# Two transformer blocks on one core: the gate steps spread over four chunks, the second output projection in alternating PSUM pairs, casts first in the inverse's chunks

## The reference

```
proj = rmsnorm(h) @ w_in_2            # q, f, i, g of HGRN2; q, k, v, z, b, a of gated delta
o_a  = hgrn2(a_q, a_f, a_i, lb)       # f = lb + (1 - lb) sigmoid(z), cumulated log f inside chunks
qkv  = silu(causal_conv(b_q, b_k, b_v)); q, k = l2norm(q), l2norm(k)
beta = sigmoid(b_b); g = -exp(A_log) * softplus(b_a + dt_bias)
o_b  = gated_delta(q, k, v, beta, g)  # needs the inverse of a unit triangular matrix per head and chunk
mix  = [rmsnorm(o_a) * silu(a_g), rmsnorm(o_b) * silu(b_z)]
h    = h + mix @ w_out_2
h    = h + peer(rmsnorm(h))           # query, top 16 of product keys, 16384 experts, computed densely
```

## Time and profile before

| | |
|---|---|
| median of 3 runs | 3259.11 us (3258.15 to 3260.24) |
| the profiled execution | 3259.25 us, of which the span is 3257.5 us |
| mean granted clock of PE | 0.994 |
| PE busy | 3207.8 us, 98% of the span |
| PEld busy | 2862.8 us, 88% |
| DVE busy | 2030.7 us, 62% |
| ACT busy | 1470.3 us, 45% |
| POOL busy | 501.8 us, 15% |
| block 2 in the trace | about 1135 to 1719 us |

### The profile page before, as it was taken

One profiled execution on the slowest core, in us unless ns is written; L12 is line 12 of the kernel. 1 busy time (PEld: TensorE's weight loads), 2 busy tenths in 40 slices (PEclk: granted clock), 3 DMA queues, 4 the chain that ended last, 5 costly groups with the idle time before them and its releaser, 6 DMA issues.

```text
span 3257.5 us, 48209 instructions
## 1 busy us (share of the span) xinstructions
PE 3207.8 (98%) x19974; PEld 2862.8 (88%) x19974; DVE 2030.7 (62%) x1833; ACT 1470.3 (45%) x1289; POOL 501.8 (15%) x418
## 2 busy tenths in 40 slices
PE   8999999999999999999999999999999999999998
PEld 7788899999999878878879999999999888888886
DVE  5455665565555656766356888999974555555554
ACT  6564453344444363464435444555544433333333
POOL 0000000000000002226300000989940000000000
PEclk9999999999999999999999999999999999999999
DMA  7444465555555443343245566676776666556663
GB/s 272 155 155 159 164 225 192 193 193 193 193 192 191 146 168 124 122 156 116 91 155 214 200 214 220 225 250 235 249 259 248 238 244 252 227 230 258 234 243 116
DMA packets 132117, 644.18 MB, mean 198 GB/s; under 512 B 14720, under 2 KB 47872, under 8 KB 62848
## 3 DMA queue, kind: packets, MB, share of 16 engines
q1 hardware_dynamic: 96592, 624.08, 53.0%
q10 hardware_dynamic: 35376, 17.94, 1.9%
HBM read 606.31 MB, written 35.66 MB: 197 GB/s over the span
## 4 chain that ended last, share of the span: by engine, by line
PE 94%; DVE 3%; ACT 2%; issue 1%; DMA 1%; SPq 0%; DVEq 0%; ACTq 0%
PE pj L293 12%; PE pj L292 12%; PE pj L294 12%; PE pj L280 7%; PE pj L279 7%; PE pj L278 7%; PE pj L1743 3%; PE pj L1745 3%; PE pj L1744 3%; PE pj L877 3%; PE pj L879 3%; PE pj L878 3%; PE pt L280 2%; PE pm L280 2%; PE pm L279 2%; PE pt L279 2%
## 5 line engine op out<-in xcount | busy, mean ns | idle before, releaser
L260 ACT ACTIVATE hi<-raw 128x2048 fp32r<-128x2048 f32 x534 | 1023.4, 1917 | 1367.2 <-PE pj L294 640.7
L267 DVE TENSOR_TENSOR lo<-raw,hi 128x2048 fp32r<-128x2048 f32 x400 | 918.4, 2296 | 678.9 <-ACT hi L260 678.1
L292 PE MATMUL pj<-xh,hi 128*128 128x256 f32 x3328 | 919.9, 276 | 0.0
L293 PE MATMUL pj<-xl,hi 128*128 128x256 f32 x3328 | 918.8, 276 | 0.0
L294 PE MATMUL pj<-xh,lo 128*128 128x256 f32 x3328 | 918.8, 276 | 0.0
L293 PEld LDWEIGHTS pj<-xl,hi 128*128 128x128 f32 x3328 | 624.9, 188 | 0.6
L292 PEld LDWEIGHTS pj<-xh,hi 128*128 128x128 f32 x3328 | 624.7, 188 | 0.6
L294 PEld LDWEIGHTS pj<-xh,lo 128*128 128x128 f32 x3328 | 624.7, 188 | 0.0
L267 DVE TENSOR_TENSOR lo_in<-raw,hi 128x2048 fp32r<-128x2048 f32 x134 | 309.3, 2310 | 266.0 <-ACT hi L260 265.3
L2431 POOL TENSOR_SCALAR hotA<-cst,slotT 128x128 fp32r<-128x128 f32 x256 | 338.2, 1337 | 473.6 <-ACT slotT L2274 437.3
L1743 PE MATMUL pj<-hi,xh 128*128 128x512 f32 x576 | 236.5, 411 | 13.4 <-ACT proj L1812 7.3
(11 more groups left out here) (397 smaller groups left out, 4267.3 us busy)
## 6 DMA issues: line engine op xcount, KB each, us to landing
raw<-w_peer SPq DMA_DIRECT2D x256, 1024.0 KB, 6.3
raw<-w_mlp SPq DMA_DIRECT2D x128, 1024.0 KB, 4.8
raw<-w_in SPq DMA_DIRECT2D x102, 1024.0 KB, 4.8
raw<-w_out SPq DMA_DIRECT2D x32, 1024.0 KB, 4.8
raw<-w_q SPq DMA_DIRECT2D x16, 1024.0 KB, 4.9
act_scratch<-hidU SPq DMA_DIRECT2D x32, 512.0 KB, 2.9
gates_scratch<-stage ACTq DMA_DIRECT2D x8, 2048.0 KB, 17.0
hidV<-act_scratch SPq DMA_DIRECT2D x32, 512.0 KB, 3.7
```

The source lines that it names most:

```text
L260: nc.scalar.activation(hi[:, j, :], raw[:, j, :], ACT.Copy).then_inc(hi_ready, 1)
L267: nc.vector.tensor_tensor(low(q)[:, j, :], raw[:, j, :], hi[:, j, :].bitcast(F32), ALU.subtract).then_inc(lo_ready, 1)
L292: nc.tensor.matmul(o, hi[:, j, cols], xh[:, k0 + k, :], start=clears, stop=False, skip_group_check=True)
L293: nc.tensor.matmul(o, hi[:, j, cols], xl[:, k0 + k, :], start=False, stop=False, skip_group_check=True)
```

## The change

It moves steps between chunks, changes the order of steps inside chunks, and gives the second output projection a second PSUM pair.

- Gates: DVE's first gate step no longer waits for ACT's sigmoid but goes first. ACT loads one table set that holds Exp and Ln (`preload_act_table_set`) behind the sigmoid in k = 10 and does gate part 1 and the first logarithm there; masks and the second logarithm move to k = 12. DVE does gate part 1 and the first split at the top of k = 11, the second split at k = 13. PE waits for the last gate step (`g_step` 6) at the fourth HGRN step and not at the first.
- `K_TILE_FIRST` (k = 11 and 39): ACT evacuates tile 0 before it casts.
- L2 norms: all of them in k = 39, the sum before DVE's lo.
- Inverse (k = 49 to 56): ACT's cast and DVE's lo come first in the iteration; the evacuation of tile 0 comes behind the first copy of a level.
- Output projection 2: groups 3, 5 and 7 use `pj[0]`; from group 3 on PE waits for the sums of one group earlier. Part 2 of the lift comes at o = 6 and part 3 at o = 7 (PE), o = 7 and 8 (ACT, DVE); part 3 is turned in `pm`. `mix_dve` part 1 comes before DVE's lo of k = 61.
- The stages after it name the two pairs the other way round.

```diff
@@
-                return (pm, pm, pt, pj[0])[b]
+                return (pm, pm, pt, pm)[b]
@@ hgrn_pe, part 0 and 1
-                    pe.wait_ge(g_step, 6)
                 hg_step(i, ((2, products), (0, transposes), (0, decay_sums)))
             else:
+                if i == 3:
+                    pe.wait_ge(g_step, 6)
                 hg_step(i, ((3, sum_v),))
@@ gates
             if part == 0:
                 act.wait_ge(wt_out, 2)
+                act.wait_ge(g_step, 1)
...
                 dve.wait_ge(wt_out, 2)
-                dve.wait_ge(g_step, 1)
@@ block2_pe
+        def block2_pair(k):
+
+            return pj[0] if k < 4 or (k - K_IN2) // 2 in (3, 5, 7) else pj[1]
...
-                    ready = ((out2_first, o // 2), (out2_second, o // 2))
+                    before = o // 2 if o < 6 else o // 2 - 1
+                    ready = ((out2_first, before), (out2_second, before))
+                if o == 6:
+                    ready = ((f_dve, 3), (f_dve, 4))
...
-                if o == 7:
-                    pe.wait_ge(mg_step, 4)
-                    lift_pe(pe, 4, 2, proj2)
-                    lift_pe(pe, 4, 3, proj2)
+                if o in (6, 7):
+                    if o == 6:
+                        pe.wait_ge(mg_step, 4)
+                    lift_pe(pe, 4, o - 4, proj2)
@@ block2_act
                 if k == K_GATE + 1:
                     gates_act(act, n, 0)
-                if k == K_GATE + 2:
+                    nc.scalar.preload_act_table_set(LOG_EXP)
+                    gates_act(act, n, 1)
                     log_forget_act(act, n, 0)
+                if k == K_GATE + 3:
+                    masks_act(act)
                     log_forget_act(act, n, 1)
-                    masks_act(act)
-                    gates_act(act, n, 1)
...
-                if k == K_L2 + 1:
+                if k == K_L2:
                     l2_act(act, n)
...
+                    if i == 3 * (k - K_LEVEL) + 1 and k > K_LEVEL and k % 4 == 3 and k < K_IN2:
+                        evacuate(k // 4, 0)
...
+                inverse = K_LEVEL < k <= K_IN2
+                if inverse:
+                    c = Q_IN2 * SLOTS + k + 2
+                    make_hi(act, c // SLOTS, c % SLOTS)
                 if k % 4 == 0 and 8 <= k <= K_IN2:
                     evacuate(k // 4 - 1, 1)
...
-                if o in (8, 9):
-                    lift_act(act, 4, o - 6, head_gain, Q_OUT2 * SLOTS)
+                if o in (7, 8):
+                    lift_act(act, 4, o - 5, head_gain, Q_OUT2 * SLOTS)
...
+                if k in K_TILE_FIRST:
+                    evacuate(k // 4, 0)
@@ block2_dve
+                    gates_dve(dve, n, 0)
+                if k == K_GATE + 2:
+                    gates_dve(dve, n, 1)
+                    split_dve(dve, 0)
+                if k == K_L2:
+                    l2_dve(dve, n, 0)
...
-                if k == K_GATE + 1:
-                    gates_dve(dve, n, 0)
-                if k == K_GATE + 3:
-                    split_dve(dve, 0)
+                if k == K_GATE + 4:
                     split_dve(dve, 1)
-                    gates_dve(dve, n, 1)
...
-                if k in (K_L2, K_L2 + 1):
-                    l2_dve(dve, n, k - K_L2)
+                if k == K_L2:
+                    l2_dve(dve, n, 1)
...
+                if k == K_STATE + 3:
+                    mix_dve(dve, n, 1)
+                inverse = K_LEVEL < k <= K_IN2
+                if inverse:
+                    c = Q_IN2 * SLOTS + k + 2
+                    make_lo(dve, c // SLOTS, c % SLOTS)
                 if o in (-2, -1):
                     lift_dve(dve, 4, o + 2, head_gain)
...
-                if o in (8, 9):
-                    lift_dve(dve, 4, o - 6, head_gain)
+                if o in (7, 8):
+                    lift_dve(dve, 4, o - 5, head_gain)
@@ later stages
-        v_pair = [pt, pm, pj[0], pj[1]]
+        pq_ = [pj[1], pj[0]]
+        v_pair = [pt, pm, pq_[0], pq_[1]]
```

More of the change, by code:

```diff
@@ L43 @@
 NEG = -30000.0
+LOG_EXP = "natural_log_exp_and_others"
 W1 = 6 * H * HD
@@ L72 @@
 K_GATE, K_HGRN, K_CONV, K_L2, K_OPS, K_LEVEL, K_STATE = 9, 13, (33, 34, 35, 36, 37, 38, 40, 41, 42), 39, 43, 48, 58
+K_TILE_FIRST = (K_GATE + 2, K_L2)
 Q_END = Q_V + PEER_SB
@@ L1733, in dense @@
                 q, j, k0, first, last = block2_chunk(k)
-                pair = pj[0] if k < 4 else pj[1]
+                pair = block2_pair(k)
                 pe.wait_ge(lo_ready, q * SLOTS + j + 1)
@@ L1879, in block2_act @@
                     lift_act(act, 4, o + 2, head_gain, (Q_OUT2 - 1) * SLOTS + o + 3)
-                if o in (8, 9):
-                    lift_act(act, 4, o - 6, head_gain, Q_OUT2 * SLOTS)
+                if o in (7, 8):
+                    lift_act(act, 4, o - 5, head_gain, Q_OUT2 * SLOTS)
                 if o in (14, 15):
                     lift_act(act, 5, o - 14, column(S_GFFN), (Q_OUT2 + 1) * SLOTS + 3 + o - 14)
-                if k >= 1:
+                if k in K_TILE_FIRST:
+                    evacuate(k // 4, 0)
+                if k >= 1 and not inverse:
                     c = Q_IN2 * SLOTS + k + 2
                     make_hi(act, c // SLOTS, c % SLOTS)
-                if k % 4 == 3 and 4 <= k < K_IN2:
+                if k % 4 == 3 and 4 <= k < K_IN2 and not inverse and k not in K_TILE_FIRST:
                     evacuate(k // 4, 0)
@@ L1947, in beside @@
                     state_squares_dve(dve, n, 0)
-                if k in (K_STATE + 2, K_STATE + 3):
-                    mix_dve(dve, n, k - K_STATE - 2)
+                if k == K_STATE + 2:
+                    mix_dve(dve, n, 0)
             def add(o, t):
@@ L1957, in add @@
                 part = resid[:, t, g * NB:(g + 1) * NB]
-                nc.vector.tensor_tensor(part, part, pj[1][:, t, :], ALU.add).then_inc((out2_first, out2_second)[t], 1)
+                nc.vector.tensor_tensor(part, part, block2_pair(K_IN2 + o)[:, t, :], ALU.add).then_inc((out2_first, out2_second)[t], 1)
             for k in range(K_ALL):
@@ L2059, in query_pe @@
                         pe.wait_ge(tp_l, 4 * n + j + 1)
-                    multiply_up(pe, Q_WQ + g, j, pj[g % 2], 4 * j, j == 0, j == SLOTS - 1)
+                    multiply_up(pe, Q_WQ + g, j, pq_[g % 2], 4 * j, j == 0, j == SLOTS - 1)
                     if g == 0 and j == 0:
@@ L2075, in router_act @@
                     act.wait_ge(r_S, b - 1)
-                nc.scalar.activation(qT[b % 2][:, :, :], up_view(pj[b % 2]), ACT.Copy).then_inc(wq_evac, 1)
+                nc.scalar.activation(qT[b % 2][:, :, :], up_view(pq_[b % 2]), ACT.Copy).then_inc(wq_evac, 1)
             if j == 2:
@@ L2244, in up_block @@
                 for j in range(SLOTS):
-                    multiply_up(pe, s + Q_PEER, j, pj[par], 4 * j, j == 0, j == SLOTS - 1)
+                    multiply_up(pe, s + Q_PEER, j, pq_[par], 4 * j, j == 0, j == SLOTS - 1)
                     if is_block(s, 0) and j == 1:
@@ L2364, in scale_up @@
                     dve.wait_ge(u_out[par], (s - (2 + par)) * 8 + 16 if not isinstance(s, int) else 16 * (s // 2))
-                nc.vector.tensor_tensor(hidU[par][:, :, :], up_view(pj[par]), rs_rowU[:, :].unsqueeze(1).broadcast_to([P, 4, TT * P]),
+                nc.vector.tensor_tensor(hidU[par][:, :, :], up_view(pq_[par]), rs_rowU[:, :].unsqueeze(1).broadcast_to([P, 4, TT * P]),
                                         ALU.mult).then_inc(u_left, 1)
```

## The result

The changed kernel takes 3229.91 us (median of 5 runs, 3228.7 to 3230.61), the kernel before 3259.02 beside it (5 runs, 3258.15 to 3260.24): a ratio of 0.9909, 95% interval 0.9899 to 0.992. 3231 was forecast, with 3226 to 3239 as the range. The profiled execution has a span of 3228.1 us, against 3257.5.

The account below looks back on a forecast made before the run. PE, busy 98% of the span, was taken to bound the kernel, so only its stops cost time. Gates 12.7, L2 norms 2.7, inverse 3.0 and projection 10.0 sum to 28.4: 3259.1 - 28.4 = 3230.7, forecast 3231 us, range 3226 to 3239.

Parts of the forecast that it names:

- Gates, 12.7: Gate stretch, k = 12 to 13: all 12.7 us that PE loses there is gained, nothing is late next.
- the loads: Gates on ACT: four table loads become one; without the preload ACT is 2.6 us later, costing 0.5 us at most.
- L2 norms, 2.7: Around k = 40 to 42: 0.7 + 4.2 us lost turn into 2.2, gain 2.7, bounds 0 and 4.9.
- two new waits for cy: Transposes after the L2 norms: PE waits 1.1 us twice, in place of one wait of 2.3; clock stays up.
- Port contention: L2 stretch: DVE casts beside POOL lose 0.15 us in each of four steps, 0.6 us, inside the bounds.
- Inverse, 3.0 out of 3.4: k = 49 to 56: casts first bring copy and update earlier; gain 3.0 of 3.4 us lost, bounds 0 and 3.4.
- Output projection 2, 10.0: Second output projection: waits for adds and xl go, all 10.0 us gained, bounds 6 and 10.0.
- the spare times: Output projection 2: lo(63) is ready 2.4 us before PE wants it, mg_step 3.8 us before.
- New waits in the middle: L2 norms and inverse give nothing, or one lift still waits and lowers the clock: 3236 to 3240, chance 0.17.
- the gates kept their gain: Against the rival that the gate stretch only moves: half of 12.7 stays, 3237 us, chance 0.05.
- the third rival: Output projection 2: alternating pairs make PE pause and the clock fall from k = 62, up to 3286 us, chance 0.03.
- DMA was no limit: Against the rival that raw chunks become the limit once PE no longer pauses: within 0.2% of before, chance 0.04.

Follow-up runs that it names:

- before_again: The kernel before, unchanged, profiled a second time: 3255.0 us (one run).
- gates_only: The kernel before with the gate steps' part of the change alone: 3245.39 us, ratio 0.9962 to the kernel before.
- no_l2: The changed kernel with the L2 norms placed as in the kernel before: 3230.86 us, ratio 0.9919 to the kernel before.
- no_inverse: The changed kernel with the inverse's chunks in the old order, casts behind the level's work: 3232.44 us, ratio 0.9925 to the kernel before.
- late_mix: The changed kernel with `mix_dve` part 1 behind lo again in iteration k = 61: 3228.58 us, ratio 0.9909 to the kernel before.
- no_pairs: The changed kernel with one PSUM pair in output projection 2 and the old waits: 3236.04 us, ratio 0.9936 to the kernel before.

## Why the prediction was right, step by step

The time was right within 1.1 us. The sum of four terms, 28.4, came out as 30.45 in the traces, less the 1.0 by which `tail` happened to start later; the medians differ by 29.1. So part of the closeness is luck: all the three terms other than the gates were too small, by 2.1 us together, and the start of `tail`, which the change does not touch, took half of that back.

Two numbers of the working don't add up, and nothing hangs on them: the waits of the earlier trace rows give 20.7 us and not 20.5, and the forecast's own range, worked out from the stated bounds (22.7 to 31.0 us gained), is 3228 to 3236 and not 3227 to 3235.

**Gates, 12.7: measured 12.69**, in the full change and alone. The mechanism held: in the changed kernel ACT's rows stand where it put them, all about 1 us later as the trace is there:

```profile
1199.76 1.28 ACT L1850 ACT_TABLE_LOAD   x1
...
1202.85 1.06 ACT L1187 ACTIVATE split<-proj 128x1024 fp32r<-128x1024 f32 x1
1204.79 0.69 ACT L1822 ACTIVATE proj<-pj,stat 128x512 f32<-128x512 f32 x1 [0.87 <-PE pj L1752]
1205.37 1.90 ACT L262 ACTIVATE hi<-raw 128x2048 fp32r<-128x2048 f32 x1
1207.53 0.69 ACT L1822 ACTIVATE proj<-pj,stat 128x512 f32<-128x512 f32 x1 [0.26 <-PE pj L1752]
```

Both evacuations wait for PE, not PE for them. What each of the gate steps' moves is worth by itself was not run, but for the preload. What the prediction said of the loads was off: with the preload dropped ACT makes one more load in chunk 10, not two, and the cost is 0, where up to 0.5 was allowed for.

**L2 norms, 2.7: measured 3.0**, but made otherwise. The two new waits for cy were forecast and came, smaller: by starts 0.76 and 0.82 us and not 1.1 each (the list has 0.6 each). DVE's rows run in the order that the prediction followed, sum, lo, scalings, lo, taps:

```profile
1419.05 2.29 DVE L1403 TENSOR_REDUCE dn<-dsq 128x16 f32<-128x2048 f32 x1
...
1421.93 2.29 DVE L269 TENSOR_TENSOR lo_in<-raw,hi 128x2048 fp32r<-128x2048 f32 x1 [0.39 <-ACT hi L262]
...
1424.63 2.37 DVE L1411 TENSOR_TENSOR proj<-proj,dn 128x1024 f32<-128x1024 f32 x2
1426.91 2.29 DVE L269 TENSOR_TENSOR lo_in<-raw,hi 128x2048 fp32r<-128x2048 f32 x1
1429.11 2.43 DVE L1359 SCALAR_TENSOR_TENSOR cy<-pj,small,cy 128x255 f32<-128x255 f32 x6
```

The shorter wait at k = 40, for tile 0, is gone as forecast; a stop of 0.3 us stands in its place at the transposes of that chunk, which begin 0.51 behind the matmul before them where 0.23 is usual. The term counted the fall of the clock, 1.6 of the 3.0 us, as the L2 part's own, and that is not shown. The fall behind the 2.3 us wait stood in both traces with the gates' long stop (before, before_again) and in neither without it (gates_only, no_l2). Beside the gate steps' change the L2 part is worth 1.4. Two against two does not show that the long stop 230 us earlier is the cause, and by which mechanism it could be stays open.

**Port contention**, counted at up to 0.6 inside the bounds, went mostly the other way. One of DVE's casts, and POOL's steps beside it:

```profile
1433.83 2.40 DVE L269 TENSOR_TENSOR lo_in<-raw,hi 128x2048 fp32r<-128x2048 f32 x1 [2.29 <-ACT hi L262]
```

```profile
1433.72 0.60 POOL L1428 TENSOR_SCALAR dgS<-cst,gt 128x128 f32<-128x128 f32 x1
1434.30 2.40 POOL L1429 TENSOR_SCALAR dkb<-proj,gt 128x128 f32<-128x128 f32 x1
1436.68 0.60 POOL L1428 TENSOR_SCALAR dgS<-cst,gt 128x128 f32<-128x128 f32 x1
```

The cast took 2.40 instead of 2.29 and lost 0.11; POOL's step that began during it took 2.40 instead of 0.60 and lost 1.8. By the Trainium skill's rule of the shared port pair (SBUF — State Buffer, SBUF: two separate sides) the one that begins second stands until the other is done. POOL's step agrees with it. The cast does not: it began 0.11 behind a POOL step that had 0.49 to go, and lost only 0.11. No wait of PE for POOL is in the list.

**Inverse, 3.0 out of 3.4: measured 4.1 and 3.9** (against before, and by no_inverse). The mechanism was right and the size too small: the measured gain is over the upper bound of 3.4. The step that was off is "of 102.0 us PE is busy 98.6, so 3.4 lost": busy time runs to the modelled end of the last matmul and so covers part of each stop. Read by starts, the four stops add up to about 3.9, and all of them went.

**Output projection 2, 10.0: measured 10.67** against the first trace of before. The mechanism was right: no wait is left, and the spare times came out as worked out. The normalisation ended 4.0 us before PE wanted it (3.8 forecast) and lo(63) 2.5 us before (2.4 forecast). late_mix shows what the new place of `mix_dve` is worth, 0.79. Two parts of the 10.67 are not due to the change, or not always. About 0.6 is the 5.60 us pace of six chunks. About 3.2 of the other 10 is clock behind the two stops, which three of four traces with these stops have and one has not (81.95 less 78.77). Against before_again the same edit brings 6.9. Of the whole, the alternating pairs carry 6.4 (no_pairs, with 1.9 of clock and what follows in it). The lift in two parts was not taken back by itself, so what it is worth is not shown.

**The rivals.** New waits in the middle came, at 0.8 us each, and did not decide; the gates kept their gain; the clock stayed at 1.00 with the pairs alternating from group 3 on, so the third rival did not come true. The Trainium skill (TensorE: Matmul & The Clock Gate, A second HAM failure mode: psum-queue depth-cycling) tells of a kernel whose clock oscillated because PE idled shortly between groups of matmuls as it cycled PSUM banks; here PE had no idle time in the projection, and alternating the pairs alone did not bring it. DMA was no limit: the last 33.6 us of the projection ran at full pace with 217 GB/s:

```profile
1656.00:1689.60 33.60, 33.60 (x160) 27.86 (x159) 19.67 (x19) 14.36 (x14) 0.00 (x0) 1.00 0.59 217
```

## What to carry to other kernels

Price a stop of PE from start to start of its instructions, not from the list of waits or from idle time: here stops of about 1 us cost a third more than was listed. Price the clock apart from the wait: whether it falls behind stops of 2 to 3 us changed from one execution of the same kernel to the next, so a gain read from one trace of before can be 3 us too large, and the gains of two edits need not add up (the gate part alone and the L2 part alone both come without the 1.6 us of clock in the convolution). When single edits are worth less than the spread of the times, cut the traces at the same instructions: stretches without a stop of over 1 us repeated within 0.2 us where whole times differed by 2.

## What the runs showed of the hardware

- The granted clock behind a stop of PE. After 6.6 us it fell in all three traces that have it, and again in all three behind the next stop, 2.0 to 2.1 us by starts for dn, some 5 us later; after 4.5 us it fell in the one trace with such a stop; after the 2.3 us for cy in two of four. In the projection it fell twice (behind the stops of 1.3 and 2.6 to 2.7 us by starts, and behind the one for xl two chunks later) in three of four traces and never in the fourth. After stops of 1.1 us or less it fell in none.
- In one execution six chunks ran at 5.60 us instead of 5.49 (0.2333 us a matmul and not 0.2288) while the granted clock stood at 1.00 and PE waited for nothing. Why stays open:

```profile
1676.35:1709.95 33.60, 33.60 (x150) 27.39 (x149) 14.85 (x15) 11.03 (x9) 0.00 (x0) 1.00 0.59 219
```

- `tail` starts between 1180.85 and 1184.81 us in fourteen traces. Ahead of it two waits of PE vary, for lo_in (6.1 to 7.9 us in all) and for qkT (6.0 to 7.7); what moves them stays open.
